# Token sums over two chunks, a turn behind the first MLP step, and samples normed by halves

## What is computed

```python
def _rmsnorm(x, g):
    y = xf * lax.rsqrt(jnp.mean(xf * xf, axis=-1, keepdims=True) + RMS_EPS)
    return (y * g.astype(jnp.float32)).astype(x.dtype)

    u = jax.nn.sigmoid(ga) * ya + jax.nn.sigmoid(gm) * ym
    x = x + _rmsnorm(u @ w_out, g_post_mix)
    h = _rmsnorm(x, g_pre_mlp)
    f = jnp.square(jax.nn.relu(h @ w_up)) @ w_down
    return x + _rmsnorm(f, g_post_mlp)
```

## Time and profile before

| | |
|---|---|
| Runs | 1088.38, 1087.61, 1085.56 us; median 1087.61 |
| Profiled execution | 1086.95 us, span 1085.4 us, granted clock 0.992 |
| TensorE, VectorE, ScalarE, POOL busy | 1048.1, 627.0, 481.9, 200.7 us |
| Share of TensorE in the chain that ended last | 78% |

### The profile page before, as it was taken

How to read it: one execution, slowest core, us unless ns; L and a number is a source line. 1 busy time by engine, 2 the same in 40 slices (tenths; PEclk the granted TensorE clock), 3 DMA queues, 4 the chain that set the end, 5 groups by cost and what they waited for, 6 DMA issues and landing times.

```text
span 1085.4 us, 20812 instructions
## 1 busy us (share of the span) xinstructions
PE 1048.1 (97%) x7523; PEld 893.1 (82%) x7523; DVE 627.0 (58%) x1239; ACT 481.9 (44%) x1026; POOL 200.7 (18%) x280
## 2 busy tenths in 40 slices
PE   7999999999999999999999998998899999999997
PEld 7988768887777877777779987996799889889985
DVE  5254445445675656665644847448477458446756
ACT  5362333324554455555543346343246236424641
POOL 4004011221001023333331100100241044024200
PEclk9999999999999999999999999999899999999999
DMA  6521224234235799999965351222332332343322
GB/s 205 157 78 50 68 59 137 69 78 127 50 88 178 211 325 330 336 338 332 339 199 157 120 182 39 69 78 68 107 88 88 106 94 83 117 115 99 108 88 87
DMA packets 114416, 153.16 MB, mean 141 GB/s; under 512 B 9597, under 2 KB 66434, under 8 KB 114322
## 3 DMA queue, kind: packets, MB, share of 16 engines
q1 hardware_dynamic: 99808, 106.98, 32.6%
q0 software_dynamic: 13120, 44.08, 12.2%
q10 hardware_dynamic: 1394, 0.83, 0.3%
HBM read 144.76 MB, written 7.10 MB: 140 GB/s over the span
## 4 chain that ended last, share of the span: by engine, by line
PE 78%; DVE 9%; DMA 5%; issue 3%; ACT 2%; SPq 2%; POOLq 0%; POOL 0%; DVEq 0%; ACTq 0%
PE ps L475 27%; PE ps L2696 12%; PE ps L925 6%; PE ps L512 6%; PE ps L483 4%; PE ps L1959 4%; DMA kring<-in_cache_k_dram 4%; PE ps L941 4%; PE ps L448 3%; PE ps L2000 1%; PE ps L1968 1%; SPq L1924 1%; PE ps L1089 1%; DVE xn L578 1%; PE ps L1109 1%
## 5 line engine op out<-in xcount | busy, mean ns | idle before, releaser
L360 DVE TENSOR_TENSOR w<-w,w 128x512 fp32r<-128x512 f32 (+1 forms) x192 | 139.5, 736 | 164.9 <-ACT w L349 159.8
L349 ACT ACTIVATE w<-w 128x512 fp32r<-128x512 f32 (+1 forms) x192 | 115.0, 608 | 196.7 <-PE ps L483 136.4
L475 PE MATMUL ps<-w,hid 128*128 128x512 f32 x672 | 164.0, 394 | 7.6 <-DVE wide L2943 7.6
L475 PEld LDWEIGHTS ps<-w,hid 128*128 128x128 f32 x672 | 127.5, 190 | 34.5 <-issue 7.9
L475 PE MATMUL ps<-w,hT 128*128 128x512 f32 x576 | 145.1, 401 | 0.0
L925 PE MATMUL ps<-hT,w 128*128 128x288 f32 x768 | 126.7, 307 | 0.0
L475 PEld LDWEIGHTS ps<-w,hT 128*128 128x128 f32 x576 | 106.0, 190 | 24.8 <-issue 3.2
L925 PEld LDWEIGHTS ps<-hT,w 128*128 128x128 f32 x768 | 105.0, 188 | 12.3 <-issue 11.6
L1926 POOL DMA_DIRECT2D vring<-in_cache_v_dram x128 | 68.8, 538 | 172.2 <-issue 172.2
L1959 PEld LDWEIGHTS ps<-ident,kring 128*128 128x128 f32 x512 | 56.6, 140 | 37.1 <-DMA kring<-in_cache_k_dram 22.9
L2130 DVE COPY kT<-ps 128x512 f32<-128x512 f32 x64 | 44.1, 689 | 74.3 <-PE ps L1959 74.3
(11 more groups left out here) (403 smaller groups left out, 1783.4 us busy)
## 6 DMA issues: line engine op xcount, KB each, us to landing
kring<-in_cache_k_dram SPq DMA_DIRECT2D x128, 256.0 KB, 4.1
vring<-in_cache_v_dram POOLq DMA_DIRECT2D x128, 256.0 KB, 4.5
w<-in_w_in_dram SPq DMA_DIRECT2D x88, 256.0 KB, 2.9
w<-in_w_down_dram SPq DMA_DIRECT2D x64, 256.0 KB, 3.0
w<-in_w_up_dram SPq DMA_DIRECT2D x40, 256.0 KB, 3.0
b<-in_w_up_dram SPq DMA_DIRECT2D x36, 256.0 KB, 3.9
w<-in_w_out_dram SPq DMA_DIRECT2D x16, 256.0 KB, 3.1
x<-in_x_prompt_dram SPq DMA_DIRECT2D x4, 512.0 KB, 7.0
```

The lines of the kernel that those rows point to most:

```text
L349: eng.activation(spread(w_hi, n, j, width), together(w32, n, j, width), ACT.Copy)\
L360: eng.tensor_tensor(spread(w_lo, n, j, width), together(w32, n, j, width), spread(w_hi, n, j, width).bitcast(F32), ALU.subtract).then_inc( ...
L475: mm = eng.matmul(ps[:, t, :], left[a][:, k, prompt_cols(t)], w[b][:, j, :], start=(k == 0 and (a, b) == THREE[0]), stop=(k == kt - 1 and ...
```

## The change

The change has four parts.

- The generator of the token sums is advanced 0, 2, 2, 2, 2, 1, 0, 0 times behind the eight weight steps of chunk 0 of the first down projection, and once behind each of the five of chunk 1. The last token high part moves from step (0, 7) to (1, 3).
- Tile 3's turn moves from the end of `pe_merge` behind the first step (first half of columns) of the MLP. The dummies ahead of tile 4's turn are 3 instead of 8. The turns use other banks, and the samples' second chunk of the output product is in bank 5 (`MIX_LAST`).
- In `act_merge` the high parts of a turn stand ahead of the norm of `x`; in `dve_merge` the low parts of the turns of tiles 1 and 2 stand ahead of `norm_tile`; both engines split the four early weight steps at tile 1, not 2.
- The samples are squared in two halves, as the prompt tiles are, and their gain is multiplied in by halves into a buffer `gained`; the sum into `x` is then one instruction.

```diff
+    gained = sb("gained", [P, D], F32, offset=at["R2"] - 2 * HALFT * 4)
-    def kept_tiles(eng, n, left, w):
+    MIX_LAST = 5
+    def kept_tiles(eng, n, left, w, last=PT):
...
-            fill(eng, n, t)
+            b_out = t if t < PT else last
+            fill(eng, n, b_out)
...
-                        mm = eng.matmul(ps[:, PT, :], left[2][:, k, T:NT + NS], w[b][:, k, :],
+                        mm = eng.matmul(ps[:, last, :], left[2][:, k, T:NT + NS], w[b][:, k, :],
...
-            filled(mm, n, t)
+            filled(mm, n, b_out)
...
-        for half, _ in enumerate(kept_tiles(eng, n, uT, wo_res)):
+        for half, _ in enumerate(kept_tiles(eng, n, uT, wo_res, MIX_LAST)):
             if half % 2 == 0 and half >= 4:
                 mixed_turn(eng, n, half // 2 - 2)
-        mixed_turn(eng, n, TILES - 2)
     def mixed_bank(e, j):
-        return (5, 6, 7, 5, 6, 7, 5, 1, 3, 7)[2 * e + j]
+        return (6, 7, 4, 0, 1, 2, 7, 3, 1, 5)[2 * e + j]
+
+    def mix_bank(t, c):
+        return MIX_LAST if t == PT and c else t
...
         def squares(t, c, e):
-            drain(eng, n, t, t == PT and c == 0, KT)
+            b = mix_bank(t, c)
+            drain(eng, n, b, t == PT and c == 0, KT)
             if t < PT:
-                eng.wait_ge(sem("mix_sq"), c * PT + e)
+                eng.wait_ge(sem("mix_sq"), c * TILES + e)
                 eng.activation(junk2[:, 0:CH], ps[:, t, :], ACT.Square, accum_out=(sq0, sq1)[c][:, t:t + 1])\
                    .then_inc(sem("mix_sq"), 1)
+                n[f"free{b}"].add()
             else:
-                eng.activation(wide[0:NS, PT, c * CH:(c + 1) * CH], ps[LOW, PT, :], ACT.Copy)\
-                   .then_inc(sem("low_part"), 1)
+                half = slice(c * CH, (c + 1) * CH)
+                eng.activation(wide[0:NS, PT, half], ps[LOW, b, :], ACT.Copy).then_inc(sem("low_part"), 1)
                 n["low_part"].add()
-            n[f"free{t}"].add()
+                n[f"free{b}"].add()
+                eng.wait_ge(sem(f"free{b}"), n[f"free{b}"].value())
+                eng.wait_ge(sem("mix_sq"), c * TILES + e)
+                eng.activation(junk2[0:NS, 0:CH], wide[0:NS, PT, half], ACT.Square,
+                               accum_out=(sq0, sq1)[c][0:NS, PT:TILES]).then_inc(sem("mix_sq"), 1)
...
             squares(t, 1, e)
-            if t < PT:
-                eng.wait_ge(sem("mix_sqe"), 1)
-            else:
-                eng.wait_ge(sem(f"free{PT}"), n[f"free{PT}"].value())
-                eng.activation(junk2[0:NS, :], wide[0:NS, PT, :], ACT.Square, accum_out=sq1[0:NS, PT:TILES])\
-                   .then_inc(sem("mix_sq"), 1)
-            eng.wait_ge(sem("mix_sq"), PT + e + 1)
-            eng.activation(rms[0:r, t:t + 1], sq1[0:r, t:t + 1], ACT.Sqrt,
-                           bias=sqe[:, t:t + 1] if t < PT else eps[0:r, :], scale=1.0 / D).then_inc(sem("mix_rms"), 1)
+            eng.wait_ge(sem("mix_sqe"), 1 if t < PT else 2)
+            eng.wait_ge(sem("mix_sq"), TILES + e + 1)
+            eng.activation(rms[0:r, t:t + 1], sq1[0:r, t:t + 1], ACT.Sqrt, bias=sqe[0:r, t:t + 1], scale=1.0 / D)\
+               .then_inc(sem("mix_rms"), 1)
...
-        eng.wait_ge(sem("mix_sq"), PT)
+        eng.wait_ge(sem("mix_sq"), TILES)
         eng.activation(sqe[:, 0:PT], sq0[:, 0:PT], ACT.Identity, bias=eps[:, :], scale=1.0 / D)\
            .then_inc(sem("mix_sqe"), 1)
+        eng.activation(sqe[0:NS, PT:TILES], sq0[0:NS, PT:TILES], ACT.Identity, bias=eps[0:NS, :], scale=1.0 / D)\
+           .then_inc(sem("mix_sqe"), 1)
         for e in range(TILES):
+            if e >= 2:
+                mixed_high(eng, n, e - 2)
             if e >= 1:
                 rms_of_x(e - 1)
-            if e >= 2:
-                mixed_high(eng, n, e - 2)
             rms_of_mixed(e)
-            if e == 2:
+            if e == 1:
                 for _ in range(EARLY_UP):
                     w_high(eng, n)
...
+            b = mix_bank(t, c)
             if t < PT:
-                eng.wait_ge(sem("mix_sq"), c * PT + e + 1)
+                eng.wait_ge(sem("mix_sq"), c * TILES + e + 1)
...
                 if c:
-                    n[f"full{t}"].add()
-                drained(eng.tensor_tensor(wide[0:NS, PT, half], ps[0:NS, PT, :], wide[0:NS, PT, half], ALU.add), n, t)
+                    n[f"full{b}"].add()
+                drained(eng.tensor_tensor(wide[0:NS, PT, half], ps[0:NS, b, :], wide[0:NS, PT, half], ALU.add), n, b)
+                eng.wait_ge(sem(f"free{b}"), n[f"free{b}"].value())
+                eng.tensor_tensor(gained[0:NS, half], wide[0:NS, PT, half], gB[0:NS, half], ALU.mult)\
+                   .then_inc(sem("mix_gain"), 1)
...
-            if t < PT:
-                eng.scalar_tensor_tensor(out=x[:, t, :], in0=wide[:, t, :], scalar=rinv[:, t:t + 1], in1=x[:, t, :],
-                                         op0=ALU.mult, op1=ALU.add).then_inc(sem("x_sum"), 1)
-            else:
-                eng.scalar_tensor_tensor(out=wide[0:r, t, :], in0=wide[0:r, t, :], scalar=rinv[0:r, t:t + 1],
-                                         in1=gB[0:r, :], op0=ALU.mult, op1=ALU.mult).then_inc(sem("mix_gain"), 1)
-                eng.wait_ge(sem("mix_gain"), 1)
-                eng.tensor_tensor(x[0:r, t, :], x[0:r, t, :], wide[0:r, t, :], ALU.add).then_inc(sem("x_sum"), 1)
+            if t == PT:
+                eng.wait_ge(sem("mix_gain"), 2)
+            eng.scalar_tensor_tensor(out=x[0:r, t, :], in0=wide[:, t, :] if t < PT else gained[0:NS, :],
+                                     scalar=rinv[0:r, t:t + 1], in1=x[0:r, t, :],
+                                     op0=ALU.mult, op1=ALU.add).then_inc(sem("x_sum"), 1)
...
         for e in range(TILES):
+            if e > 2:
+                mixed_low(eng, n, e - 2)
             if e >= 1:
                 norm_tile(eng, 1, e - 1, ORDER[e - 1], x, xn, g2B)
-            if e >= 2:
-                mixed_low(eng, n, e - 2)
+            if e == 2:
+                mixed_low(eng, n, 0)
             added(e)
-            if e == 2:
+            if e == 1:
                 for _ in range(EARLY_UP):
                     w_low(eng, n)
...
-                features_chunk(eng, n, h2T, KT, early={EARLY_UP - 1: last_turn})
+                features_chunk(eng, n, h2T, KT, early={0: lambda: mixed_turn(eng, n, TILES - 2), EARLY_UP - 1: last_turn})
...
         def last_turn():
-            keep_busy(eng, 7, 8)
+            keep_busy(eng, 1, 3)
             mixed_turn(eng, n, TILES - 1)
-            for b in (5, 1):
-                eng.wait_ge(sem(f"free{b}"), n[f"free{b}"].value())
-            keep_busy(eng, 1, 12)
-            for b in (3, 7):
-                eng.wait_ge(sem(f"free{b}"), n[f"free{b}"].value())
-
-
-        for b, later in ((5, 1), (6, 0), (7, 0)):
-            eng.wait_ge(sem(f"free{b}"), n[f"free{b}"].value() - later)
+            eng.wait_ge(sem("free3"), n["free3"].value())
+            keep_busy(eng, 3, 12)
+            eng.wait_ge(sem("free5"), n["free5"].value())
+
+        eng.wait_ge(sem("free2"), n["free2"].value())
         mlp_passes(body)
...
-    TOKEN_TURNS = ((0, 2), (0, 3), (0, 4), (0, 7))
+    TOKEN_TURNS = ((0, 2), (0, 3), (0, 4), (1, 3))
...
                     w_low(eng, n)
-                    if i == 0 and (c, k) >= (0, 1):
-                        next(tokens, None)
-                        if c == 0:
+                    if i == 0:
+                        for _ in range((0, 2, 2, 2, 2, 1, 0, 0)[k] if c == 0 else 1):
                             next(tokens, None)
```

## The result

The changed kernel took 1073.81 us (median of 4 runs, 1072.39 to 1074.91) beside 1087.73 for the kernel before (4 runs, 1085.56 to 1088.38): ratio 0.9864, 95% interval 0.9831 to 0.9897 (the quotient of the two medians is 0.9872). The profiled execution took 1074.91, with a span of 1073.3 and a granted clock of 0.994.

What follows compares the result with a forecast made beforehand. TensorE, busy for 97% of the span, was taken as the bound. 9.9 us at the chunk boundary (7.7 idle, 2.6 clock, less 0.4) plus 3.6 in the head made 13.5, so 1074.0 us, range 1071.5 to 1078.0.

Steps and rivals of the forecast that it cites:

- Boundary: Between the two chunks of the first down projection: spread token sums remove 7.7 us idle, with 0.4 charged at bank 4.
- Clock at the boundary: Chunk 1 of the first down projection: the clock's fall to 0.91 after idle time costs 2.6 us, to be regained.
- Head: Tile turns up to the second half of the columns: turn 4 at 679.3, second half at 681.2, 3.6 us gained.
- POOL: Chunk 1: POOL's four sums fall on VectorE's remaining token work, 5.2 us, under the 9.4 spare.
- A gap of 2.55 at 671 left the clock at full level: Head of the kernel before: the 48 matmuls behind the gap took 0.137 each, so a milder boundary wait is likelier.
- 0.8 to the order: Head: low and high parts ahead of the norms let norm(3) run from 671.7, not 672.51; 0.8 us gained.
- (a): Chunk boundary: VectorE is still late; 1079.4 us, or 1075.5 to 1076.8 in the milder form; chance 0.12.
- (b): Head gives nothing, its norms paced by ScalarE's and VectorE's turns among each other; 1077.7 us; chance 0.10.
- (c): Whole kernel: the change does nothing, savings return as a wait further on; about 1086 to 1088 us; chance 0.03.
- (d): First product: the tail of the token work holds the products; slower, 1092.3 us at 25 us of delay; chance 0.03.

Runs made afterwards that it cites:

- e3: Changed kernel with one token instruction fewer in chunk 0 (0,2,2,2,2,0,0,0) and 2,1,1,1,1 in chunk 1; 1073.70 us.
- e4: Changed kernel with two token instructions more in chunk 0, 11 in all, and 1,0,0,1,1 in chunk 1; 1077.06 us.
- e5: Kernel before with 64 dummy transposes into bank 7 between the two chunks of the first down projection; 1086.21 us.
- b1: Kernel before, unchanged, profiled a second time; 1088.50 us.
- b2: Kernel before, unchanged, profiled a third time; 1087.91 us.
- e1: Kernel before with only the token sums spread (9 in chunk 0, 5 in chunk 1); 1078.02 us.
- h4: Changed kernel with the old order on ScalarE and VectorE and tile 3's turn back ahead of the MLP; 1077.48 us.
- h2: Changed kernel with the old order on ScalarE and VectorE in the head, tile 3's turn still behind the first step; 1078.69 us.
- e2: Changed kernel with the token sums put back as before, so the head's changes alone; 1082.03 us.
- h3: Changed kernel with the samples squared whole and their gain in one long instruction, as before; 1078.64 us.
- h1: Changed kernel with tile 3's turn back ahead of the MLP's first step; 1076.56 us.
- h5: Kernel before with 20 dummy transposes in TensorE's gap ahead of tile 3's turn; 1086.71 us.

## Why the prediction was right

The forecast was 1074.0 with 1071.5 to 1078.0; measured 1073.81. The mechanism held in both places; that the two agree to 0.2 us is partly luck, as the points on the clock show. Point by point:

- **Boundary.** Predicted: drain from 754.83 and chunk 1 at once, then 0.4 at bank 4, chunk 1 about 25.8. Measured: the drain 0.90 ahead of chunk 1 in both, no wait at bank 0, 0.3 at the samples' bank and another 0.1 at the next weight step, chunk 1 25.88. e3 and e4 moved the drain by one and two instructions and got the waits that this margin says.
- **Clock at the boundary.** The sum had 2.6 less 0.4, so 2.2 net; by the first product's own start it is 2.40 less 0.45, 1.95 net. I had taken the end of chunk 1 before at 791.44, 0.16 too late. e5 shows that it is the clock, worth 1.9: at full clock the kernel before would have paid the 0.5 at the samples' bank too. In the profiled execution it came to that bank (768.59) only after its release (766.53 and 0.14), because its first 12 matmuls were slow. Over the three profiles of before the net sum varies from 1.1 to 1.97.

```profile
768.59 0.62 PE L483 MATMUL ps<-w,hid 128*128 128x512 f32 x2
```

- **Head.** 3.6 predicted, 3.58 measured against the same profile. On the time scale of before, norm(3) began at 672.94 - 1.19 = 671.75 (predicted 671.7), turn 4 at 679.34 (679.3), the second half at 681.27 (681.2).
- **POOL.** It ran beside the tail of the token work as said. The last low part ended 18.2 after the start of chunk 1, not 16.5, so 7.7 us were spare and not 9.4. POOL's four sums cost VectorE 1.6 (1.1 at one token sum, 0.5 at one weight step), under the 5.2 that was taken as the most.
- **One step failed**: "A gap of 2.55 at 671 left the clock at full level". It did so in that execution. Of six profiles with this gap of 2.5 (before, b1, b2, e1, e5, h4) the clock fell in four (b1, b2, e1, e5), and the head stretch of the five with the old head was 16.42, 16.94, 17.60, 17.61 and 17.44, on average 17.20. Against the average execution the head so gives 4.4, not 3.6. At the boundary the clock's net gain averages 1.7 over the three profiles of before, not the 2.2 of the sum. So 0.8 too little in the head and 0.5 too much at the boundary partly cancel: with the averages the sum is 4.4 + 7.7 + 1.7 = 13.8, beside 13.9 between the medians.
- **The account of the parts** was also thin. I put 0.8 to the order, for norm(3). That is what it did to norm(3): it began 3.32 after the turn of tile 2, and 4.08 after it in h2. But with the turn behind the first step the order does more: h2 shows that it releases that step 3.9 earlier, by the low part of tile 2. The order and the move of the turn therefore belong together; the move alone, on the old order, loses (h2 against h4).
- **Rivals.** (a) in its milder form is what e4 makes of the kernel, and 9 instructions just escape it. (b) fails by e2, (c) by e1 and e2 together, (d) by the 7.7 us to spare.

Not tried: a different number of dummies ahead of tile 4's turn, and the other banks or the earlier weight steps by themselves. What decides in which executions the clock falls stays open.

## What to carry to other kernels

Where the busiest engine waits for a drain, count the work that the draining engine has in front of it since the last point at which both orders agree. Moving whole instructions behind the drain pays their length until the drain starts before the other engine needs the bank; after that there was 0.5 left to win here (e3). When a step is moved ahead, move what releases it too: the turn behind the first step was a loss of 3.5 us under the old order (0.9 without the clock's share) and a gain of 1.4 under the new one. And one trace shows one outcome of the clock; profile the kernel before two or three times ahead of saying that a gap is free.

## What the runs showed of the hardware

The granted clock of TensorE fell from the full level (2.4 GHz) towards the half (1.2 GHz) at gaps of 1.70 us (h3, mean 0.67 behind it) and 3.73 us (h2, 0.50), and in four of six executions at a gap of 2.5 (b2, 0.79). It held at 1.00 behind gaps of 1.77 (h1) and 2.43 (e4). Each of these is one execution. A fall cost between 0.5 us (b1) and 2.6 (h2) in the head, and 1.1 (b2) to 2.3 (e2) at the boundary, where the idle time was 7.55 each time. Dummy transposes in the gap went with a clock of 1.00 behind it in e5 (64 of them) and in h5 (20). VectorE and POOL held each other up in both directions: one VectorE sum of 1.35 took 2.44, a weight step 1.21 instead of 0.69, and POOL sums of 1.29 took 1.77 and 2.41 in the same 6 us. The other rows of that time in the changed kernel:

```profile
764.28 0.69 DVE L361 TENSOR_TENSOR w<-w,w 128x512 fp32r<-128x512 f32 x1 [1.21 <-ACT w L350]
...
769.09 1.21 DVE L361 TENSOR_TENSOR w<-w,w 128x512 fp32r<-128x512 f32 x1 [1.75 <-ACT w L350]
```

```profile
764.36 1.77 POOL L2655 TENSOR_TENSOR t2s<-t1s,b 128x512 f32<-128x512 f32 x1
```

In the middle the ends follow each other by turns, some 1.2 apart: POOL 766.13, VectorE 767.34, POOL 768.49. By the Trainium skill (SBUF — State Buffer, section Who interferes with whom) a VectorE instruction with two SBUF inputs and a POOL instruction that reads SBUF contend for one port pair under an exclusive lock, so one of them waits until the other has ended. The two durations of over 2.4 agree with that: each is the instruction's own length and another 1.1, less than one instruction of the other engine.
